# Third feed-forward, first gate slab: three chunks of the residual and of the mixer output multiplied apart, and joined at the eviction

## What is computed

```python
# second_block, after both mixers
mixed = (gate_a * y_a + gate_b * y_b) @ w_out
h = h + rms_norm(mixed, mix_post_g)
u = rms_norm(h, ffn_pre_g)
gt, up = split(u @ w_ffn_in, 2)          # 2816 columns each
h = h + rms_norm((silu(gt) * up) @ w_ffn_out, ffn_post_g)
```

## Time and profile before

| | |
|---|---|
| median of 3 runs | 1019.05 us (1018.82 to 1020.08) |
| the profiled execution | 1015.89 us |
| its span, first to last instruction | 1014.2 us |
| TensorE busy, share of the span | 99% |
| VectorE busy | 69% |
| ScalarE busy | 51% |
| GpSimd busy | 10% |
| granted TensorE clock, mean | 0.999 of 2.4 GHz |

### The profile page before, as it was taken

How to read it: one execution, slowest core, us unless ns; L and a number is a source line. 1 busy time by engine, 2 the same in 40 slices (tenths; PEclk the granted TensorE clock), 3 DMA queues, 4 the chain that set the end, 5 groups by cost and what they waited for, 6 DMA issues and landing times.

```text
span 1014.2 us, 20015 instructions
## 1 busy us (share of the span) xinstructions
PE 1005.5 (99%) x8699; PEld 992.6 (98%) x8699; DVE 698.8 (69%) x697; ACT 516.3 (51%) x586; POOL 97.4 (10%) x96
## 2 busy tenths in 40 slices
PE   8999999999999999999999999999999999999997
PEld 8999999999999999999999999999999999999997
DVE  6765655777777875555679877697758777656564
ACT  7544444536737554344457566554545556444343
POOL 1000000300010200000013400110006330000000
PEclk9999999999999999999999999999999999999999
DMA  9766666475555665666554563534535537565651
GB/s 285 241 212 195 200 200 200 150 229 165 163 167 167 208 201 183 202 198 199 178 176 146 167 207 94 157 125 126 165 126 167 174 126 244 184 207 166 207 165 41
DMA packets 148383, 180.43 MB, mean 178 GB/s; under 512 B 3997, under 2 KB 135314, under 8 KB 148322
## 3 DMA queue, kind: packets, MB, share of 16 engines
q1 hardware_dynamic: 147504, 177.55, 54.8%
q0 software_dynamic: 544, 1.86, 0.7%
q10 hardware_dynamic: 274, 0.13, 0.0%
HBM read 178.47 MB, written 1.05 MB: 177 GB/s over the span
## 4 chain that ended last, share of the span: by engine, by line
PE 97%; DVE 1%; DMA 1%; ACT 0%; issue 0%; SPq 0%; DVEq 0%; ACTq 0%
PE ps L1629 30%; PE ps L1630 30%; PE ps L1631 30%; PE ps L2065 1%; DMA ar<-in_x_dram 1%; PE ps L2069 0%; PE ps L2109 0%; PE ps L1895 0%; PE ps L2041 0%; PE ps L2031 0%; PE ps L2017 0%; PE ps L2021 0%; PE ps L1883 0%; DVE ar L1621 0%; PE ps L1904 0%
## 5 line engine op out<-in xcount | busy, mean ns | idle before, releaser
L1409 DVE TENSOR_TENSOR w_lo<-stage,w_hi 128x2048 fp32r<-128x2048 f32 x164 | 379.1, 2313 | 170.8 <-ACT w_hi L1223 170.5
L1223 ACT ACTIVATE w_hi<-stage 128x2048 fp32r<-128x2048 f32 x164 | 312.5, 1907 | 158.4 <-PE ps L1631 157.6
L1629 PE MATMUL ps<-x_hi,w_lo 128*128 128x256 f32 (+1 forms) x1284 | 358.9, 280 | 0.0
L1631 PE MATMUL ps<-x_hi,w_hi 128*128 128x256 f32 (+1 forms) x1284 | 356.6, 278 | 0.0
L1630 PE MATMUL ps<-x_lo,w_hi 128*128 128x256 f32 (+1 forms) x1284 | 356.5, 278 | 0.0
L1629 PE MATMUL ps<-a_hi,w_lo 128*128 128x256 f32 (+1 forms) x1132 | 315.1, 278 | 0.3 <-DVE a_lo L1415 0.3
L1630 PE MATMUL ps<-a_lo,w_hi 128*128 128x256 f32 (+1 forms) x1132 | 313.0, 277 | 0.0
L1631 PE MATMUL ps<-a_hi,w_hi 128*128 128x256 f32 (+1 forms) x1132 | 313.0, 277 | 0.0
L1629 PEld LDWEIGHTS ps<-x_hi,w_lo 128*128 128x128 f32 x1284 | 241.2, 188 | 2.2 <-issue 1.8
L1630 PEld LDWEIGHTS ps<-x_lo,w_hi 128*128 128x128 f32 x1284 | 241.3, 188 | 0.0
L1631 PEld LDWEIGHTS ps<-x_hi,w_hi 128*128 128x128 f32 x1284 | 241.2, 188 | 0.0
(11 more groups left out here) (324 smaller groups left out, 826.7 us busy)
## 6 DMA issues: line engine op xcount, KB each, us to landing
stage<-in_w_in_dram SPq DMA_DIRECT2D x36, 1024.0 KB, 5.3
stage<-in_ffn_w_down_dram SPq DMA_DIRECT2D x22, 1024.0 KB, 5.0
stage<-in_w_ffn_in_dram SPq DMA_DIRECT2D x22, 1024.0 KB, 5.2
stage<-in_ffn_w_gate_dram SPq DMA_DIRECT2D x21, 1024.0 KB, 5.4
stage<-in_ffn_w_up_dram SPq DMA_DIRECT2D x21, 1024.0 KB, 5.4
stage<-in_w_ffn_out_dram SPq DMA_DIRECT2D x11, 1024.0 KB, 5.0
stage<-in_w_gate_dram SPq DMA_DIRECT2D x8, 1024.0 KB, 5.4
stage<-in_w_out_dram SPq DMA_DIRECT2D x8, 1024.0 KB, 5.4
```

Of the source, the lines that this page charges most:

```text
L1223: nc.scalar.activation(o, i, ACT.Copy).then_inc(s["hi_ready"], 1)
L1409: nc.vector.tensor_tensor(o, i, b.bitcast(F32), ALU.subtract).then_inc(s["lo_ready"], 1)
L1629: nc.tensor.matmul(o, wl, xh, start=start, stop=False, skip_group_check=skip)
L1631: return nc.tensor.matmul(o, wh, xh, start=False, stop=stop, skip_group_check=skip)
```

## The change

- At i = 40 ScalarE makes the fp32r part of h * ffn_pre_g for chunks 0 to 2, and at i = 41 that of mg * ffn_pre_g for the same chunks (three activations each, ahead of the weight split of that iteration). VectorE makes the rests behind its weight split of the same iteration (three instructions each). They are kept in a_hi and a_lo, chunks 2 to 4 (h) and 5 to 7 (mg), which are free until the new h is there.
- The mean of the mixer output goes to banks 0 and 1, since 4 and 5 now take products.
- `keep_busy` and its nine matmuls are gone. TensorE multiplies chunk 0 of h with G0 before the spread, chunks 1 and 2 of h after it (banks 4 and 5), then chunks 0 to 2 of mg with G0 (bank 3).
- `first_slabs` leaves those three chunks of G0 out and goes chunk by chunk instead of by pairs; the mean moves ahead of the last chunk of both slabs.
- ScalarE's a_hi of block 1 waits for the reading of the h products' rows, those of blocks 2 and 3 for the mg ones (`kick_read`). Ahead of G1's split ScalarE copies bank 3 to m_gate.
- VectorE makes the a_lo of a block before the add of the next one also for blocks 2 and 3. It scales m_gate by r ahead of G1's split, and adds the rest of G0 (banks 4 and 5) behind it; the first gate eviction reads that sum.
- TensorE's use of bank 3 for U1 waits for the copy.

```diff
@@ ScalarE, mixer2_act, iterations 39 to 41 (j = i - 39)
+                    if j:
+                        act.wait_ge(s["x2_done"], 2 * DC)
+                        act.wait_ge(s["mg_done"], APART)
+                        for c in range(APART):
+                            k = VEC["ffn_pre_g_2"] + c
+                            src, dst = (h, h_rows[0]) if j == 1 else (mg, m_rows[0])
+                            nc.scalar.activation(dst[:, c, :], src[:, c, :], ACT.Copy, scale=vec[:, k:k + 1]).then_inc(s["early_hi"], 1)
...
@@ VectorE, mixer2_dve
                     split_lo(n + i + 3)
+                if i in (40, 41):
+                    for c in range(APART):
+                        src, hi, lo = (h, *h_rows) if i == 40 else (mg, *m_rows)
+                        dve.wait_ge(s["early_hi"], APART * (i - 40) + c + 1)
+                        k = VEC["ffn_pre_g_2"] + c
+                        nc.vector.scalar_tensor_tensor(out=lo[:, c, :], in0=src[:, c, :], scalar=vec[:, k:k + 1],
+                                                       in1=hi[:, c, :].bitcast(F32), op0=ALU.mult, op1=ALU.subtract).then_inc(s["early_lo"], 1)
...
                 nc.vector.tensor_tensor(v, v, bc(r, 2), ALU.mult).then_inc(s["mg_scaled"], 1)
-                if b == 1:
-                    input_lo(0, g, 32, (a_hi, a_lo), chunks=(1,))
+                input_lo(b - 1, g, 32, (a_hi, a_lo), chunks=(1,) if b == 1 else (0, 1))
                 dve.wait_ge(s["mg_scaled"], b + 2)
                 nc.vector.tensor_tensor(hb, hb, v, ALU.add).then_inc(s["h_new"], 1)
-                if b > 1:
-                    input_lo(b - 1, g, 32, (a_hi, a_lo))
             input_lo(3, g, 32, (a_hi, a_lo))
+            dve.wait_ge(s["mg_done"], 9)
+            dve.wait_ge(s["h_new"], 17)
+            nc.vector.tensor_tensor(pair(ga_s), pair(m_gate), bc(r, 2), ALU.mult).then_inc(s["mg_scaled"], 1)
             split_lo(n + 45)
+            dve.wait_ge(s["slab_used"], n + 44)
+            dve.wait_ge(s["mg_scaled"], 6)
+            nc.vector.tensor_tensor(pair(ga_s), pair(ga_s), ps[:, 4:6, 0:SEQ], ALU.add).then_inc(s["mg_scaled"], 1)
...
@@ ScalarE, input_hi and the seam
+                    if early:
+                        act.wait_ge(s["kick_read"], (3, 4, 4)[b - 1])
...
-            input_hi(a_hi, g, 16, (1, 2, 3))
+            input_hi(a_hi, g, 16, (1, 2, 3), early=True)
+            act.wait_ge(s["kick_read"], 4)
+            nc.scalar.activation(m_gate, ps[:, 3, :], ACT.Copy).then_inc(s["mg_done"], 1)
             split_hi(N_FFN[2] + 2)
...
@@ TensorE, first_slabs
                     for k in ks:
+                        if j == 0 and k < apart:
+                            continue
...
-                for k in range(0, DC - 2, 2):
-                    part(0, (k, k + 1))
-                    part(1, (k, k + 1))
+                for k in range(0, DC - 2, 1 if apart else 2):
+                    ks = (k,) if apart else (k, k + 1)
+                    if k >= apart:
+                        part(0, ks)
+                    part(1, ks)
+                if apart:
+                    part(0, (DC - 2,))
+                    part(1, (DC - 2,))
+                    mean()
+                    part(0, (DC - 1,)).then_inc(s["slab_used"], 1)
+                    part(1, (DC - 1,)).then_inc(s["slab_used"], 1)
+                    return
...
@@ TensorE, end of mixer2
-                        last = nc.tensor.matmul(ps[:, 4 + t, SEQ:SEQ + 2], v[:, P * t:P * t + P], ones[:, 0:2],
+                        last = nc.tensor.matmul(ps[:, t, SEQ:SEQ + 2], v[:, P * t:P * t + P], ones[:, 0:2],
                                                 start=j == 0, stop=j == 2)
                 last.then_inc(s["mean_done"], 1)
-                keep_busy(1, 2)
+                def apart(outs, src, k, first_bank=True):
+                    for c in range(2):
+                        w = slice(P * c, P * c + P)
+                        last = products(outs[c], gate_hi[:, k, w], gate_lo[:, k, w], src[0][:, k, :], src[1][:, k, :],
+                                        k == 0 and (c == 0 or first_bank), False, skip=True)
+                    return last
+
+                n3 = N_FFN[2]
+                gate_hi, gate_lo = wview(w_hi, n3, DC), wview(w_lo, n3, DC)
+                slab_ready(n3)
+                pe.wait_ge(s["mg_done"], 8)
+                pe.wait_ge(s["early_lo"], APART)
+                h_out = [ps[:, 4, 0:SEQ], ps[:, 5, 0:SEQ]]
+                apart(h_out, h_rows, 0)
                 pe.wait_ge(s["rstd_ready"], 8)
                 for i in range(NT):
                     last = nc.tensor.matmul(ps[:, 0, P * i:P * i + P], rcol[:, 1, i:i + 1].to_broadcast([P, P]), ident[:], start=True, stop=True)
                 last.then_inc(s["spread"], 1)
-                keep_busy(1, 7)
+                for k in range(1, APART):
+                    last = apart(h_out, h_rows, k)
+                last.then_inc(s["kick_read"], 1)
+                pe.wait_ge(s["early_lo"], 2 * APART)
+                for k in range(APART):
+                    last = apart(halves(3), m_rows, k, first_bank=False)
+                last.then_inc(s["kick_read"], 1)
```

More of the change, by code:

```diff
@@ L122 @@
 gsigb_done gsiga_done merged2 kick_ffn kick_hi kick_lo kick_read m2_hi m2_lo mg_done msq_done out_first mg_scaled spread h_first
+early_hi early_lo
 """.split()
@@ L256, in program @@
         yp, pgb = view(4096, 4, 512), view(6144, D)
+        APART = 3
+        h_rows, m_rows = ([v[:, c:c + APART, :] for v in (a_hi, a_lo)] for c in (2, 5))
+        m_gate = view(12800, 512)
         K0 = P + META
@@ L1226, in squares, with input_hi @@
                 nc.scalar.activation(sq[:, 2 * b:2 * b + 2, :], h[:, 2 * b:2 * b + 2, :], ACT.Square).then_inc(s["sq_done"], 1)
-            def input_hi(dst, g, base, bs=range(4), late=False):
+            def input_hi(dst, g, base, bs=range(4), late=False, early=False):
                 for b in bs:
                     act.wait_ge(s["h_new"], base + b + 1)
+                    if early:
+                        act.wait_ge(s["kick_read"], (3, 4, 4)[b - 1])
                     for c in (2 * b, 2 * b + 1):
@@ L1353, in _ @@
             mixer2_act(act, split_hi, load_table)
-            root(5, ps[:, 4:6, SEQ], rcol[:, 0, 0:2], loaded=True)
+            root(5, ps[:, 0:2, SEQ], rcol[:, 0, 0:2], loaded=True)
             g = vec[:, VEC["ffn_pre_g_2"]:]
@@ L1427, in ffn @@
                 n, J0 = N_FFN[f], PAIRS * f
-                first_gate = ps[:, 2:4, 0:SEQ] if f == 0 else ps[:, 4:6, 0:SEQ]
+                first_gate = (ps[:, 2:4, 0:SEQ], ps[:, 4:6, 0:SEQ], pair(ga_s))[f]
                 first_up = pair(ps[:, 0, :]) if f == 0 else ps[:, 6:8, 0:SEQ]
@@ L1432, in gate_out @@
                     dve.wait_ge(s["slab_used"], up(m + 1, it))
+                    if first and f == 2:
+                        dve.wait_ge(s["mg_scaled"], 7)
                     nc.vector.tensor_tensor(pair(ga_s), first_gate if first else pair(ps[:, J % 2, :]), bc2,
@@ L1688, in second_slab, with first_slabs @@
                 last.then_inc(s["slab_used"], 1)
-            def first_slabs(n, outs, srcs, base, mean, late=False):
+            def first_slabs(n, outs, srcs, base, mean, late=False, apart=0):
                 def part(j, ks):
@@ L1763, in late_mean @@
                 nc.tensor.matmul(o, ones[:], sq[:, DC - 1, :], start=False, stop=True).then_inc(s["mean_done"], 1)
-            def keep_busy(bank, count):
-                for _ in range(count):
-                    nc.tensor.matmul(ps[:, bank, 0:SEQ], ones[:], tab[:, T_COS:T_COS + SEQ], start=True, stop=True)
             def token_sums(k, squares_done):
@@ L1797, in upward @@
                         pe.wait_ge(s["up_scaled"], up(max(J - 1, 1), it, 2))
+                        if f == 2 and J == J0 + 1:
+                            pe.wait_ge(s["mg_done"], 9)
                     feature_slab(m, halves(2 + J % 2), ffn_input(f), it=it)
@@ L1804, in ffn @@
                     first_slabs(n, [[ps[:, 4 + 2 * j, 0:SEQ], ps[:, 5 + 2 * j, 0:SEQ]] for j in range(2)], [ffn_input(f)] * 2, base,
-                                lambda: mean_mm(norm, ps[:, 2 + J0 % 2, 0:SEQ]).then_inc(s["mean_done"], 1))
+                                lambda: mean_mm(norm, ps[:, 2 + J0 % 2, 0:SEQ]).then_inc(s["mean_done"], 1), apart=APART if f == 2 else 0)
                 for b in range(2):
```

## The result

| | before | after |
|---|---|---|
| median of 22 runs each, alternating on one chip | 1018.97 us | 1020.36 us |
| ratio, 95% interval | | 1.0016 [1.0009, 1.0022] |
| the profiled execution, its span | 1015.89, 1014.2 us | 1019.63, 1017.9 us |

What follows compares the result with a forecast made beforehand. It took the ScalarE and VectorE chain at the seam between mixer and third feed-forward as the bound: 0.97 at G1 plus 0.1 behind, called +1.0 us on 1019.05, gives 1020.05 us; range 1017.8 to 1021.4.

Steps and rivals of the forecast that it cites:

- ScalarE late by three activations: Before the seam, at iteration 41: three added activations (1.22 us) start the last square 0.96 us late, at 820.90.
- The hole in TensorE: In the mixer's mean: the second four of its eight matmuls start 0.77 us later, with nothing to fill the gap.
- First scaling: VectorE's first scaling in the seam: about 0.8 us later, at 823.38 for 822.58.
- The new order: VectorE's adds behind two a_lo each, with GpSimd contention: block-3 add ends at 832.6 for 830.72.
- G1: Third feed-forward's first slab: first product 6.25 us after the block-3 add, at 838.85, +0.97 us; TensorE waits 1.1 us.
- Behind it: After G1's start: VectorE's 5.35 us of work against TensorE's 5.43 us slab window, level; charged 0.1 us.
- TensorE's work decides: Rival in the seam: ScalarE and VectorE keep up and TensorE's smaller work sets the time; -1.2 us, 1017.85; chance 0.15.
- Contention: Rival in the seam: VectorE-GpSimd lock also hits the first round; end +3.1 us, 1022.15; chance 0.12.
- The clock: Rival: without fillers TensorE's idle gaps drop its clock to 1.2 GHz; 3.5 us more, 1023.5; chance 0.03.

Runs made afterwards that it cites:

- e1: Changed kernel with the rows of h made at i = 39 and of mg at i = 40, one iteration sooner; ratio to before 1.0005.
- e7: Changed kernel with all six rows of h and mg made at i = 41, ahead of the last split; ratio to before 1.0042.
- e3: Changed kernel with ScalarE's w_hi of G1 right behind the first root and VectorE's w_lo ahead of the scaling of m_gate; ratio to before 1.0031.
- e2: Changed kernel with VectorE's old order in blocks 2 and 3, add first, then a_lo of the block before; ratio to before 1.0007.
- e5: Changed kernel with the rows of h and mg one iteration sooner and G1's w_hi behind the first root; ratio to before 0.9991.
- e4: Kernel before without its nine filler matmuls, nothing else changed; ratio to before 0.9999.
- e6: Changed kernel with the rows one iteration sooner and VectorE's old order in blocks 2 and 3; ratio to before 0.9996.
- e12: Changed kernel with two filler matmuls covering TensorE's wait ahead of the mixer's mean; ratio to before 1.0013.
- e10: The e5 kernel run a second time, on another chip; ratio to before 0.9990.

## Why the prediction was right

Times of after are less 1.77 here, to stand in the frame of the earlier trace rows.

- *ScalarE late by three activations*: last square at 820.86, forecast 820.90. Right; e1 takes it away, e7 more than doubles it. The hole in TensorE lies ahead of the first matmul of the mean, which waits for the square of chunk 6, and not where I put it, ahead of the second four; it is 0.86 us long, and those four are 1.09 late, foreseen as 0.77.
- *First scaling*: 823.53, forecast 823.38.
- *The new order*: block-3 add ends at 832.90, forecast 832.6, with the block-1 and block-3 adds at 1.23 beside GpSimd and the block-2 add at 0.68, as foreseen. By the Trainium skill, SBUF — State Buffer, section SBUF: two separate sides, the forecast was 832.6, without its rule 832.1; the trace agrees with the rule, and e3 shows it at its longest here, 1.9 us on GpSimd. What the order costs at G1 is 0.5 us (e2), less than the two a_lo that stand ahead of each add, since it also removes waits for a_lo (1.16 and 0.58 in e2, 0.50 in the kernel after).
- *G1*: from that add to G1's first product 6.21 us, forecast 6.25 (the terms as listed add to 6.22); the first product at 839.11, +1.23, forecast +0.97; the wait there 0.92, forecast 1.1.
- *Behind it*: the one term that was mis-sized. I charged 0.1; it is 0.72 (1.95 less 1.23). VectorE did keep up, as I argued: TensorE has no wait there. The cost is the pitch, 144 products at 0.118 for 0.113. I had taken 5.43 us for a slab as fixed, although show 0.118 in the seam. Why the pitch changes stays open. So both terms came out larger than forecast, 1.23 for 0.97 and 0.72 for 0.1. The 1.95 of the profiled executions lies above my own range of +0.1 to +1.6; the 1.6 of the medians, with 0.9 to 2.2 around it, lies at its edge. The mechanism up to G1 was right; that the total still came inside the range owes something to luck.
- *The rivals*: "TensorE's work decides" is refuted by the four waits; even with the rows and G1's w_hi out of the way (e5) G1 comes 0.63 earlier, not 1.2. "Contention" happened as far as the forecast had it and no further. "The clock" was under-rated as an event and over-rated as a price: I gave it 0.03 and +3.5 us; it falls in one to two of three executions and costs the first scaling 0.5 to 0.6 us where it covers the spread (e3, e7). It fell 1.2 us behind a wait of 2.04 us (e7), 1.4 us behind one of 2.28 and 2.1 us behind one of 0.64 (both e3), and not behind one of 0.64 in e2. The Trainium skill, TensorE: Matmul & The Clock Gate, section HAM oscillation, warns of the clock being lost in gaps between bursts of matmuls; the runs agree that it is, here with no gap over 2.3 us, and show that a fall costs next to nothing where it comes behind the spread and VectorE sets the pace (e4).

The seam's sum by the runs: 1.1 us at G1 for the place of mg's rows (e1), 0.3 for the order (e1 to e6), less 0.15 for the spread without fillers ahead of it (e6 to before), +1.23; and 0.7 behind it for the pitch. That is 1.95 in the profiled execution, and the interval of the medians is 0.9 to 2.2: the runs don't need a price of the clock besides, nor can they exclude one.

## What to carry to other kernels

Useful work in place of fillers gains nothing if the wait that the fillers cover is set by other engines, and what prepares that work lands in their queues: here three activations in the one stretch where ScalarE had no slack cost 1.1 us, and an iteration earlier nothing that shows. Before a long VectorE operation is pulled ahead, look at what GpSimd is about to start: the one that began second was held up by the first, GpSimd by 1.9 us in e3, VectorE by 0.4 in e5. And compare distances from a common event inside the program, not spans: executions of one kernel lie 4 us apart, while the distances in the seam came out alike to 0.01 us in both pairs of profiles that can be compared.

## What the hardware showed that I had not expected

- The same stream of 256-column fp32r products runs at one of two steady pitches, 0.113 or 0.118 us, for 3 to 50 us at a time, at granted clock 1.00 and with no idle time. Ahead of the seam the pitch of one stretch differs between executions of the same code (after and e12); behind it two profiled executions of one kernel (e5, e10) are alike to 0.01 us. The cause was not found: not VectorE's order alone, not the wait at G1, not a small matmul between.
- Whether the clock falls behind a wait of 0.6 to 0.9 us differs between executions: 7 of 21 after at a mean of 0.997, and e3's profile against e2's. A mean of 0.998 does not tell, since the clock falls at the end of every program here. TensorE at clock 0.50 for 3.7 us and more, at a pitch of 0.21 us, changed the time of the whole program by nothing that could be measured (e4).
- After a wait, at clock 1.00, the first product costs 0.19 us to the next one for the usual 0.113 to 0.118 (in every such wait in the seam of these profiles), so a wait costs 0.08 us more than its length.
